# Loading the next head pair's keys, values and bias earlier in an attention stage that also streams a key/value cache

## The reference

```
PATTERNS = ((128, 1), (512, 4), (2048, 16))          # (window, dilation), 16 heads of 64

# prompt: q, k, v of 1024 positions, computed by this layer's own projection
res = [dilated_band(q, k, v, d, w // d) for (w, d) in PATTERNS]
#   s = q k^T * Dh**-0.5 - slope[h] * distance;  p = exp(s - max);  o = p v / sum(p)
o = combine_patterns([r[0] for r in res], [r[1] for r in res])

# samples: 8 sequences, keys and values = 2048 cached positions + 8 new ones
kall = concatenate([cache_k[i], kn], axis=1); vall = concatenate([cache_v[i], vn], axis=1)
res = [dilated_gather(qs, kall, vall, d, w // d) for (w, d) in PATTERNS]
os_ = combine_patterns(...)
```

## Time and profile before

| | us |
|---|---|
| median of three runs | 3007.02 |
| lowest and highest run | 3002.83, 3007.36 |
| the profiled execution: its own time | 3007.36 |
| the profiled execution: its span | 3005.5 |
| the profiled execution: TensorE busy in the span | 2901.9 (97%) |
| the attention stage, from its first bias load to the first weight block behind it | about 1591.6 to 2086.2 |

### The profile page before, as it was taken

How to read it: one execution, slowest core, us unless ns; L and a number is a source line. 1 busy time by engine, 2 the same in 40 slices (tenths; PEclk the granted TensorE clock), 3 DMA queues, 4 the chain that set the end, 5 groups by cost and what they waited for, 6 DMA issues and landing times. The chain is left out here.

```text
span 3005.5 us, 47421 instructions
## 1 busy us (share of the span) xinstructions
PE 2901.9 (97%) x21301; PEld 2758.6 (92%) x21301; DVE 1358.1 (45%) x1742; ACT 784.6 (26%) x1240; POOL 142.2 (5%) x230
## 2 busy tenths in 40 slices
PE   7999999999999999999997999998999999999997
PEld 6998999999999999999995676776999999999997
DVE  5753435434433444745502555556343444344433
ACT  5443423111111111322214444544221111111110
POOL 1010000000000000200001111110000000000000
PEclk9999899999999999999997999999999999999999
DMA  5120131111111111132228666763111111111111
GB/s 185 43 65 17 36 109 43 43 56 43 43 43 43 43 43 43 43 128 81 83 89 279 223 205 214 257 208 129 57 43 43 43 43 43 43 43 43 43 42 60
DMA packets 122123, 253.81 MB, mean 84 GB/s; under 512 B 7554, under 2 KB 83542, under 8 KB 121409
## 3 DMA queue, kind: packets, MB, share of 16 engines
q1 hardware_dynamic: 107648, 184.83, 19.1%
q0 software_dynamic: 12960, 61.42, 6.0%
q10 hardware_dynamic: 1312, 4.52, 0.4%
HBM read 222.72 MB, written 28.02 MB: 83 GB/s over the span
## 5 line engine op out<-in xcount | busy, mean ns | idle before, releaser
L221 PE MATMUL psum<-h_hi,w_hi 128*128 128x364 f32 x2592 | 575.3, 330 | 11.1 <-DVE h_lo L287 10.1
L221 PE MATMUL psum<-h_hi,w_lo 128*128 128x364 f32 x2592 | 573.4, 330 | 0.0
L221 PE MATMUL psum<-h_lo,w_hi 128*128 128x364 f32 x2592 | 573.2, 329 | 0.0
L221 PEld LDWEIGHTS psum<-h_hi,w_hi 128*128 128x128 f32 x2592 | 450.6, 188 | 14.1 <-issue 11.3
L221 PEld LDWEIGHTS psum<-h_hi,w_lo 128*128 128x128 f32 x2592 | 451.6, 188 | 0.0
L221 PEld LDWEIGHTS psum<-h_lo,w_hi 128*128 128x128 f32 x2592 | 450.4, 189 | 0.0
L204 ACT ACTIVATE w_hi<-w_raw 128x2048 fp32r<-128x2048 f32 x96 | 183.6, 1913 | 676.1 <-PE psum L221 627.6
L456 PE MATMUL psum<-w_hi,h_hi 128*128 128x256 f32 (+1 forms) x1152 | 327.7, 284 | 3.9 <-DVE h_lo L287 3.9
L456 PE MATMUL psum<-w_hi,h_lo 128*128 128x256 f32 (+1 forms) x1152 | 325.2, 282 | 0.0
L456 PE MATMUL psum<-w_lo,h_hi 128*128 128x256 f32 (+1 forms) x1152 | 324.3, 282 | 0.0
L1458 DVE TENSOR_TENSOR x_res<-x_res,psum 128x1092 f32<-128x1092 f32 x176 | 227.3, 1291 | 207.6 <-PE psum L221 207.6
(11 more groups left out here) (317 smaller groups left out, 3145.4 us busy)
## 6 DMA issues: line engine op xcount, KB each, us to landing
cache_tile<-in_cache_k SPq DMA_DIRECT2D x64, 512.0 KB, 8.5
cache_tile<-in_cache_v SPq DMA_DIRECT2D x64, 512.0 KB, 6.5
w_raw<-in_w_ffn_gate SPq DMA_DIRECT2D x22, 1024.0 KB, 5.1
w_raw<-in_w_ffn_up SPq DMA_DIRECT2D x22, 1024.0 KB, 5.1
w_raw<-in_w_ffn_down SPq DMA_DIRECT2D x22, 1024.0 KB, 4.9
w_raw<-in_w_in_att SPq DMA_DIRECT2D x12, 1024.0 KB, 7.1
w_raw<-in_w_in_rec SPq DMA_DIRECT2D x10, 1024.0 KB, 5.1
park_x<-x_res POOLq DMA_DIRECT2D x2, 4368.0 KB, 13.7
```

The costliest lines, as they stand in the source:

```text
L221: mm = pe.matmul(PS[:, bank + c, 0:CW], st[:, slot, wc:wc + P], mv[:, k, c * CW:(c + 1) * CW], start=(i < NCH), stop=(i >= 3 * NCH * nk - ...
```

## The change

Only `s9_pool` changes, in three conditions. `load_b(p + 1)` moves from block 5 to block 1, `load_v(p + 1)` from block 6 to block 2, and `load_qk(p + 2)` from block 4 to block 3. The waits ahead of each load, their sizes, their buffers and their number stay the same.

```diff
             if s == 6 and b + 1 < DB:
                 q_blocks(b + 1)
             if p and p + 1 < HP:
-                if qb == 5:
+                if qb == 1:
                     pool.wait_ge(a_red, 16 * p)
                     load_b(p + 1)
-                if qb == 6:
+                if qb == 2:
                     pool.wait_ge(a_o, 8 * p)
                     load_v(p + 1)
-            if qb == 4 and p + 2 < HP:
+            if qb == 3 and p + 2 < HP:
                 bank, count = qk_last(p + 1)
                 pool.wait_ge(t_in[bank], count)
                 load_qk(p + 2)
```

## The result

The changed kernel took 3024.44 us, the median of 6 runs (3017.19 to 3029.45), against 3007.68 us for 6 runs of the kernel before on the same chips: a ratio of 1.0052, 95% interval 1.0034 to 1.0069. It is slower by about 16.8 us. The profiled execution took 3031.2 us (span 3029.4), some 7 us over the median of its kernel, so its sums are a little large.

A forecast was written before the change was run, and what follows sets the result against it. The prediction took TensorE, busy 97% of the span, as the bound. Values 8.4, bias 1.2 and clock 1.7 us sum to 11.3 us on the profiled 3007.36, giving 3018.7, set at 3018 us; range 3008 to 3031 us.

The forecast's parts named there:

- Where the wait sits, and that it is the only one: After block 3's scores, pairs 1 to 6, TensorE waits for key tiles before transposing; 1.85 us idle in pair 3.
- the one place: The key-tile wait was claimed as a period's only place where a transfer is on TensorE's path; 5.3 us in all.
- No gain from clearing blocks 4 to 6: Block 4 to the next pair's block 1 takes about 34.65 us whichever loads are there, so clearing gains 0.
- POOL pays nothing: In blocks 1 to 3 the waits before the moved loads are already met, and their issue fits POOL's idle time.
- The bias in block 1, 1.2 us, and queries and keys in block 3, 0 us: Bias tail meets value tiles 8 and 9, 0.2 us for each of 6 pairs; queries and keys are hidden behind key tiles.
- The values, 8.4 us: Issued in block 2 together with key tile 0, they delay it 1.4 us in each of six pairs.
- the two prices: Key tile 0's delay in block 2: 1.3 us by transfer rate, or 2.3 us by a tile issued behind `att_v`.
- The clock, 1.7 us: Longer key-tile waits bring one short fall of TensorE's clock, 3.4 us at half clock, losing 1.7 us.
- a rival with 0.13 chance: Clock falls behind the longer waits in most pairs; 3027 to 3030 us for short falls, over 3050 for long; chance 0.13.
- The total: Whole kernel: 11.3 us added to the profiled 3007.36 us gives 3018.7, prediction set at 3018 us.

The follow-up runs named there:

- e3: Against the changed kernel: the values are loaded in block 3 instead of block 2, ahead of queries and keys; 3008.40 us, ratio 1.0003 to the kernel before.
- e2: Against the changed kernel: the values go back to block 6, bias and query/key loads stay moved; 3009.67 us, ratio 1.0010 to the kernel before.
- e5: Against the changed kernel: 7 extra products on TensorE just before its wait for key tile 0, pairs 1 to 6; 3015.07 us, ratio 1.0034 to before.
- e10: Against the changed kernel: 7 extra products before the key tile 0 wait, run again beside the changed kernel on one chip; 3019.00 us, 1.0038 to before.
- e9: The changed kernel unaltered, run again on one chip beside the kernel with 7 extra products; 3025.85 us, ratio 1.0055 to the kernel before.
- e1: Against the kernel before: only the value load moves, from block 6 to block 2; 3020.45 us, ratio 1.0042.
- e6: Against the kernel before: value load cut in two, token blocks 0 to 3 in block 2, the rest in block 6; 3012.72 us, ratio 1.0029.
- e7: Against the kernel before: only the bias load, 1024 KB, moves, into block 2; 3024.91 us, ratio 1.0070.
- e8: Against the kernel before: GpSimd instead of SP issues the four small loads of value tile 9 in block 1; 3016.92 us, ratio 1.0042.
- e11: Against the kernel before: ScalarE instead of SP issues value tile 9's four small loads at the end of block 1; 3007.11 us, ratio 0.9993.

## Why the prediction was right, by its own steps

- **Where the wait sits, and that it is the only one.** Right for the place: the new loss lies in blocks 2 and 3 of pairs 1 to 6, and e3 shows that one block further the same load is free. Not right for "the one place": the earlier trace rows already had 4.6 us of waits for value tiles, and in pair 4 after it is the last value tile that TensorE stands waiting for, 3.31 us.
- **No gain from clearing blocks 4 to 6.** Right: 34.65 us again in pair 1, and e2 gains nothing.
- **POOL pays nothing.** Right: the issues fall into its idle time, and the `att_diag` of block 2 starts 9.17 us behind that of block 1 after (1816.35 - 1807.18), 9.16 before.
- **The bias in block 1, 1.2 us, and queries and keys in block 3, 0 us.** Together 3.1 us measured in e2 (interval 0.3 to 6 us), so right within what can be told. Which of the two it is, or whether it is the one clock fall in pair 7, stays open.
- **The values, 8.4 us, with the bias's 1.2 a sum of 9.6 us for the waits.** Near, as far as the runs can tell: where the clock is nearly out of it, the medians are 9.5 us (e5) and 8.8 us (e10) over before, which holds what is left of the clock's share and any excess of the added products over the waits. Single executions show more, 15.5 us of longer waits in the profiled one and 13.6 us (11.3 + 12.2 - 9.9) in that of e9, but both were the slowest of their kernel. I had put nearly all of it on key tile 0; part falls on the last value tiles, whose waits grew by 3.5 and 7.6 us in these two. One of the two prices had a weaker base than I said: the tile of the earlier trace rows was not without a load near, since the bias load of the earlier trace rows was under way until 2015.1 us. A tile asked for at 2030.7 us, with none near, landed in 3.6 us, so the price hardly changes.
- **The clock, 1.7 us.** This term was mis-sized, by a factor of about four. I allowed one fall; there were six in the profiled execution, and by e9 against e10 the clock carries about 6.9 us of the loss, by longer busy time 9.1 us in the profiled execution. What I had made a rival with 0.13 chance (falls in most pairs, short kind) is in fact a part of what happened. The rival's own time, 3027 to 3030 us, took 9.6 us for the waits and 10 for the clock and lies just above the measured median.
- **The total.** 3018 us against 3024.4: the clock's term, low by 5.2 us, makes most of the difference. The range, 3008 to 3031 us, held the time, and the sign was as forecast. The misses did not cancel: they lie on the same side.

## What to carry to other kernels

Whether a prefetch can be moved earlier for nothing is decided by what it delays there; the free slots of the issuing engine say nothing of that, and nor does a full transfer share by itself: block 3, where the load was free, has a share of 1.04 already before. Before moving one, look for the transfer that an engine already stands waiting for, and keep other loads a slot away from its issue: here the same 512 KB cost 14 us in block 2 and nothing in block 3 or block 6. And when a wait of TensorE grows by a microsecond or two in each round of a loop, count the granted clock too.

## What the runs showed that was not expected

The clock's share is nearly as large as the waits'. The table gives, for the profiled execution of each, TensorE's waits for cache tiles over the 9.9 us of before, and the time at granted clock 0.50 between 1640 and 2080 us, of which at most half is lost; before had none. Single executions differ in both.

| | longer waits, us | at half clock, us | median over before, us |
|---|---|---|---|
| changed kernel | 15.5 | 23.9 | 16.8 |
| changed kernel again (e9) | 13.6 | 27.3 | 15.7 |
| values only (e1) | 6.3 | 13.7 | 13.9 |
| all but values (e2) | 1.8 | 3.4 | 3.1 |
| values in block 3 (e3) | 0.3 | 3.4 | 1.9 |
| half the values (e6) | 3.0 | 10.2 | 7.2 |
| bias in block 2 (e7) | 10.5 | 17.1 | 19.4 |
| tile 9 by GpSimd (e8) | 4.9 | 17.1 | 11.4 |
| tile 9 by ScalarE (e11) | -0.6 | 3.4 | -3.1 |

Longer waits come with more falls, but the length of one wait does not decide whether a fall follows. In the kernel before, waits of 1.85 and 2.33 us had none behind them. In e1 a wait of 1.85 us at the same place had one; the value-tile wait just ahead of it was 0.80 us there, 0.36 before. In the changed kernel the waits of 2.7 to 4.2 us of pairs 1 to 6 each had one, of 3.4 us or twice that, and one of 2.69 us in pair 7 had none. What decides between them was not tested. The Trainium skill ("TensorE: Matmul & The Clock Gate", section "HAM oscillation — how this bites in real kernels") describes a loop that loses its clock at each wait for a transfer, and the changed kernel's trace agrees, with a fall in each of the pairs 1 to 6. Extra work put into such a wait, 7 products, lowered the median by 6.9 us, and with 14 of them, 3.39 us against waits of 2.7 to 4.2 us, nothing was gained.

A load issued by another engine is not the same load: with value tile 9 issued by GpSimd the value-tile waits rose from 4.6 to 14.4 us, issued by ScalarE to 8.5 us, and the medians were 11.4 us over and 3.1 us under before.
